# Front of a decoder-layer kernel: x tiles and weight blocks queued behind one another, six x tiles scaled on the vector engine

## What is computed

```
def rms_norm(x, g):
    y = xf * lax.rsqrt(jnp.mean(xf * xf, axis=-1, keepdims=True) + NORM_EPS)
    return (y * g.astype(jnp.float32)).astype(x.dtype)
...
u = rms_norm(h, norm_mix[i])
parts = jnp.split(u @ w_in[i], IN_OFFSETS, axis=-1)
q_n, kc, vc, ks_, vs_, kw, vw, gate_n, q_f, k_f, v_f, f_l = parts
o_n = nsa_attention(...)       # compressed, selected and window branches
o_f = forgetting_attention(...)
y = g_a * (o_n @ w_branch_nsa[i]) + g_b * (o_f @ w_branch_fox[i])
h = h + y @ w_out[i]
h = h + jnp.square(jax.nn.relu(v @ w_up[i])) @ w_down[i]
return rms_norm(h, norm_final)
```

## Time and profile before

| | us |
|---|---|
| time, median of 3 runs | 1181.09 (1180.12 to 1181.48) |
| time of the profiled execution | 1180.81 |
| its span on the slowest core (core 5) | 1179.2 |
| spans of the eight cores | 1175.8 to 1179.2 |
| PE busy | 1126.7 (96% of the span) |
| DVE busy | 653.2 (55%) |
| ACT busy | 623.1 (53%) |
| end of the front's last matmul on core 5 | 89.5 |

### The profile page before, as it was taken

One profiled execution on the slowest core, in us unless ns is written; L12 is line 12 of the kernel. 1 busy time (PEld: TensorE's weight loads), 2 busy tenths in 40 slices (PEclk: granted clock), 3 DMA queues, 4 the chain that ended last, 5 costly groups with the idle time before them and its releaser, 6 DMA issues.

```text
span 1179.2 us, 25453 instructions; the slowest of 8 cores (1175.8 to 1179.2 us)
## 1 busy us (share of the span) xinstructions
PE 1126.7 (96%) x8735; PEld 610.7 (52%) x8735; DVE 653.2 (55%) x1482; ACT 623.1 (53%) x1264; POOL 73.0 (6%) x136
## 2 busy tenths in 40 slices
PE   3888989999999999999999999999999999999997
PEld 2455655676575757644444455444444444444443
DVE  2555767655545455544344466356556564747377
ACT  4755888999999999932222366321111212030354
POOL 1000222122110000000000000000000000000000
PEclk9999999999999999999999999999999999999999
DMA  9963000002020034182032222312212111222034
GB/s 201 200 149 62 5 10 9 8 6 44 9 37 6 3 54 83 30 268 36 11 62 36 53 38 46 80 37 36 37 36 37 36 36 36 36 36 37 1 123 164
DMA packets 19228, 65.86 MB, mean 56 GB/s; under 512 B 4416, under 2 KB 5184, under 8 KB 15136
## 3 DMA queue, kind: packets, MB, share of 16 engines
q0 software_dynamic: 5184, 34.15, 16.8%
q1 hardware_dynamic: 13920, 30.08, 8.1%
HBM read 89.38 MB, written 8.39 MB: 83 GB/s over the span
## 4 chain that ended last, share of the span: by engine, by line
PE 89%; DMA 4%; DVE 3%; issue 2%; ACT 1%; DVEq 0%; POOL 0%; ACTq 0%; POOLq 0%; SPq 0%
PE bank L328 89%; DMA RG<-x 4%; DVE RG L328 2%; ACT RG L328 1%; POOL RG L328 0%; DVEq L167 0%; DVE arena L328 0%; DVEq L160 0%; DVE uT L328 0%; ACTq L167 0%; POOLq L167 0%; SPq L167 0%
## 5 line engine op out<-in xcount | busy, mean ns | idle before, releaser
L328 ACT ACTIVATE RG<-bank 128x512 bf16<-128x512 f32 (+3 forms) x888 | 452.0, 618 | 336.4 <-PE bank L328 331.5
L328 PE MATMUL bank<-uT,arena 128*128 128x512 bf16 x2048 | 490.3, 379 | 1.3 <-DVE arena L328 0.9
L328 PE MATMUL bank<-RG 128*128 128x65 bf16 (+8 forms) x3780 | 323.7, 225 | 14.0 <-DVE RG L328 11.2
L328 PEld LDWEIGHTS bank<-uT,arena 128*128 128x128 bf16 x2048 | 199.4, 98 | 213.4 <-issue 1.7
L328 DVE TENSOR_TENSOR RG<-RG,bank 128x512 f32<-128x512 f32 x320 | 218.9, 687 | 144.7 <-PE bank L328 141.5
L328 PE MATMUL bank<-arena,RG 128*128 128x512 bf16 x1280 | 279.5, 379 | 0.0
L328 PEld LDWEIGHTS bank<-RG 128*128 128x128 bf16 (+3 forms) x3780 | 198.7, 97 | 106.8 <-issue 21.9
L328 DVE TENSOR_TENSOR RG<-RG 128x512 bf16<-128x512 f32 (+3 forms) x199 | 118.3, 595 | 154.5 <-ACT RG L328 150.5
L328 PEld LDWEIGHTS bank<-arena,RG 128*128 128x128 bf16 x1280 | 124.8, 98 | 148.1
L328 ACT ACTIVATE RG<-RG 128x512 f32<-128x512 f32 (+3 forms) x149 | 86.8, 586 | 75.6 <-DVE RG L328 46.4
L328 ACT ACTIVATE RG<-bank,prm_s 128x512 f32<-128x512 f32 x64 | 43.9, 687 | 117.5 <-PE bank L328 114.8
(11 more groups left out here) (40 smaller groups left out, 296.8 us busy)
## 6 DMA issues: line engine op xcount, KB each, us to landing
arena<-wall POOLq DMA_DIRECT2D x30, 1024.0 KB, 9.8
RG<-x SPq DMA_DIRECT2D x32, 512.0 KB, 16.6
out<-RG SPq DMA_DIRECT2D x32, 256.0 KB, 2.1
RG<-c_qx SPq DMA_DIRECT2D x8, 144.0 KB
arena<-wall POOLq DMA_DIRECT2D x4, 256.0 KB, 16.1
RG<-wall POOLq DMA_DIRECT2D x1, 1024.0 KB, 13.9
arena<-wall POOLq DMA_DIRECT2D x1, 576.0 KB, 10.8
RG<-c_kx SPq DMA_DIRECT2D x4, 144.0 KB
```

Source lines behind the costliest of these rows:

```text
L328: return P.emit(eng, lambda e, method=method, kw=kw: getattr(e, method)(**kw), ins, outs, inc)
```

## The change

The x tiles are issued one by one by `load_x`. x1 goes ahead of the parameters. KV is issued once x3 has landed; x4 (and what stands behind it on SP) waits for the first piece of KV. QN waits for x10, x12 waits for QN, W1K waits for x12 with W1V behind it, and the constants wait for W1K. `stageA` and `stageB` run one tile less ahead. For tiles 0 to 5 the scale moves from ACT to DVE. Ln takes its epsilon from a small tile filled by a memset in place of `prm`. All four `kv_group`s of the first four tiles go in one piece (`room = 99.0` at i = 3), the later ones follow right behind their fourth tile, and qn groups move to tile 9 and on.

```diff
+        load_x(0)
+        W.pump(n=1)
+        load_x(1)
+        P.dma('sp', prm[:, :], prm_d)
+        load_x(2)
+        load_x(3)
...
+        E('dve', 'memset', ap=epsb[:, :], constant=1e-6)
...
-        E('dve', 'tensor_copy', out=w2b, in_=prm[:, 112:240])
-        E('dve', 'tensor_copy', out=posb[0:64, :], in_=prm[0:64, 48:112])
+        W.pump(n=2, after=[x_tok[3]])
+        load_x(4, [W.toks[1]])
+        load_x(5)
...
+            if i < 6:
+                E('dve', 'tensor_scalar', out=xn[i % 4], in0=xs[b], scalar1=rstd[:, i:i + 1], scalar2=None, op0=ALU.mult)
+            else:
+                E('act', 'activation', out=xn[i % 4], in_=xs[b], func=AF.Copy, scale=rstd[:, i:i + 1])
...
         stageA(0)
         stageB(0)
+        load_x(6)
         stageA(1)
-        stageB(1)
-        stageA(2)
         todo = []
         for i in range(16):
-            if i + 3 < 16:
-                stageA(i + 3)
             if i + 2 < 16:
-                stageB(i + 2)
-            if i == 4:
-                P.dma('pool', w1kb, wall_d[BLK['W1K']], after=[x_tok[7]])
+                stageA(i + 2)
+            if i + 1 < 16:
+                stageB(i + 1)
+            if i + 7 < 16:
+                load_x(i + 7, [W.toks[5]] if i == 5 else [])
+            if i == 3:
+                W.pump(n=3, after=[x_tok[10]])
             if i == 6:
-                W.pump(n=4, after=[x_tok[9]])
-            if i == 12:
-                late_consts()
+                w1k_tok = P.dma('pool', w1kb, wall_d[BLK['W1K']], after=[x_tok[12]])
+                W.pump(n=4)
+            if i == 9:
+                late_consts([w1k_tok])
             stageC(i)
+            if i == 8:
+                E('dve', 'tensor_copy', out=w2b, in_=prm[:, 112:240])
+                E('dve', 'tensor_copy', out=posb[0:64, :], in_=prm[0:64, 48:112])
             tg = i // 4
-            if i > 0:
+            if i % 4 > 0:
                 todo.append((1.0, lambda i=i: tm_group(i - 1)))
-            if i == 3 or i in (8, 12):
-                tg = (i - 1) // 4
+            if i % 4 == 3:
                 todo += [(1.73, lambda j=j, tg=tg: kv_group(tg, j)) for j in range(4)]
...
+                todo.append((1.0, lambda i=i: tm_group(i)))
...
-            room = 4.2
+            room = 99.0 if i == 3 else 4.4
```

More of the change, by code:

```diff
@@ L341, in build_program @@
         prm = sbt('prm_s', [128, 249], F32)
+        epsb = sbt('epsb', [128, 16], F32)
         RG_BYTES = 143552
@@ L375, in __init__ @@
                 self.released = set()
+                self.toks = []
             def slot_ap(self, pos):
@@ L385, in pump @@
                     for c0, c1 in PIECES.get(nm, [(0, 4096)] if nm in BLK else []):
-                        P.dma('pool', self.slot_ap(pos)[:, c0:c1], wall_d[BLK[nm], :, c0:c1], after=after)
+                        tok = P.dma('pool', self.slot_ap(pos)[:, c0:c1], wall_d[BLK[nm], :, c0:c1], after=after)
+                        self.toks.append(tok)
                     self.loaded += 1
@@ L465, in build_program, with load_x @@
         x_tok = []
[L466 to L473, removed]
+        def load_x(i, after=()):
+            x_tok.append(P.dma('sp', xs[i % NXS], x_d[i * 128:(i + 1) * 128, :], after=after))
+        load_x(0)
[4 more added lines that the diff above has]
+        load_x(3)
+        E('pool', 'memset', ap=identb[:, :], constant=1.0)
+        E('pool', 'affine_select', out=identb[:, :], in_=identb[:, :], pattern=[[1, 128]], compare_op=ALU.is_equal, fill=0.0, base=0, channel_multiplier=-1)
         for ap in (vall, fv0):
@@ L481, in build_program, with late_consts @@
         E('dve', 'memset', ap=ss, constant=0.0)
+        E('dve', 'memset', ap=epsb[:, :], constant=1e-6)
         E('act', 'activation', out=rstd[:, 0:1], in_=ss[:, 0, 0:1], func=AF.Ln, bias=1.0)
-        E('dve', 'tensor_copy', out=w2b, in_=prm[:, 112:240])
-        E('dve', 'tensor_copy', out=posb[0:64, :], in_=prm[0:64, 48:112])
-        def late_consts():
-            P.dma('sp', identf[:, :], cd['c_identf'])
+        W.pump(n=2, after=[x_tok[3]])
+        load_x(4, [W.toks[1]])
+        load_x(5)
+        def late_consts(after):
+            P.dma('sp', identf[:, :], cd['c_identf'], after=after)
             P.dma('sp', trib[:, :], cd['c_tri'])
@@ L535, in stageB @@
             tb = 3 + i % 3
-            E('act', 'activation', out=rstd[:, i:i + 1], in_=ss[:, i, 0:1], func=AF.Ln, scale=1.0 / D, bias=prm[:, 240:241])
+            E('act', 'activation', out=rstd[:, i:i + 1], in_=ss[:, i, 0:1], func=AF.Ln, scale=1.0 / D, bias=epsb[:, 0:1])
             E('act', 'activation', out=rstd[:, i:i + 1], in_=rstd[:, i:i + 1], func=AF.Exp, scale=-0.5)
-            E('act', 'activation', out=xn[i % 4], in_=xs[b], func=AF.Copy, scale=rstd[:, i:i + 1])
+            if i < 6:
+                E('dve', 'tensor_scalar', out=xn[i % 4], in0=xs[b], scalar1=rstd[:, i:i + 1], scalar2=None, op0=ALU.mult)
+            else:
+                E('act', 'activation', out=xn[i % 4], in_=xs[b], func=AF.Copy, scale=rstd[:, i:i + 1])
         def stageC(i):
@@ L571, in build_program @@
         stageB(0)
+        load_x(6)
         stageA(1)
[L573 to L574 removed]
         todo = []
         for i in range(16):
[L577 to L578 removed]
             if i + 2 < 16:
[L580 to L582 removed]
+                stageA(i + 2)
[5 more added lines that the diff above has]
+                W.pump(n=3, after=[x_tok[10]])
             if i == 6:
[L584 to L586 removed]
+                w1k_tok = P.dma('pool', w1kb, wall_d[BLK['W1K']], after=[x_tok[12]])
+                W.pump(n=4)
+            if i == 9:
+                late_consts([w1k_tok])
             stageC(i)
+            if i == 8:
+                E('dve', 'tensor_copy', out=w2b, in_=prm[:, 112:240])
+                E('dve', 'tensor_copy', out=posb[0:64, :], in_=prm[0:64, 48:112])
             tg = i // 4
[L589 removed]
+            if i % 4 > 0:
                 todo.append((1.0, lambda i=i: tm_group(i - 1)))
[L591 to L592 removed]
+            if i % 4 == 3:
                 todo += [(1.73, lambda j=j, tg=tg: kv_group(tg, j)) for j in range(4)]
[L594 to L596 removed]
+                todo.append((1.0, lambda i=i: tm_group(i)))
+                if tg == 1:
+                    todo += [(1.73, lambda c=c, tg=tg: qn_group(0, c, tg, ('act', 'dve'), front_bank)) for tg in range(2) for c in range(2)]
+            room = 99.0 if i == 3 else 4.4
             while todo and room > 0:
@@ L602, in build_program @@
             fn()
-        tm_group(15)
-        for j in range(4):
-            kv_group(3, j)
         W.release(pos_kv)
```

2 lines of the change are left out of this document (removed).

## The result

The changed kernel takes 1189.75 us (median of 6 runs) against 1181.21 for the kernel before (6 runs): ratio 1.0072, 95% interval 1.0060 to 1.0083. It is slower by 8.5 us, outside the range of the forecast (1177.8 to 1186.0). The profiled execution took 1190.03, 1.6 above the span of its slowest core, as before.

The account below looks back on a forecast made before the run. Late x transfers held the front, with 8.5 us of PE waits. Core 5: front end 88.5 plus 1089.7 gives 1178.2; slowest core 1180.6, plus 1.6 and 0.3, gives 1182.5 us; range 1177.8 to 1186.0.

Parts of the forecast that it names:

- The working's last step: Sum over cores: core 5 at 1178.2, core 0 at 1181.1, slowest core 1180.6, time 1182.5.
- Term 1: Start of front: x3 lands at 15.5, KV is issued then, its first piece takes 4.5 and lands at 20.0.
- Term 2: x4, issued at 20.0 behind KV's first piece: 3.7 alone plus 1.5 for neighbours, landing at 25.2 (bounds 23.7 and 27.4).
- Term 3: From x4's landing through ACT and DVE steps to the first kv group: 6.3, start at 31.5, a loss of 3.1.
- Term 4: PE waits behind the first kv group: 2.7 up to 46.8, then 0.7; 3.4 against the old 8.5.
- Term 5: PE's lower clock in the first kv groups: loss of 1.0, bounds 0 and 3.5; core 5's front ends at 88.5.
- What was to cost nothing: Later W1K, W1V, QN, constants, FOX0, SP's waits, memsets and casts: covered by other work, no cost beyond terms 1 and 2.
- (c): Rival, slower: idling ahead of tile 3 leaves PE at 1.2 GHz through four kv groups, price 3.5; 1185.8, chance 0.25.
- the sign for (c) at the end of the prediction: Sign in the new profile: the first kv groups take 7 us more than 7.
- (b): Rival, the order pays: x4 at 23.7, no lower clock, fewer waits, front end 85.0; 1178.6, chance 0.20.
- (a): Rival: the later start (3.1) and the removed waits (5.1) cancel on every core; 1181, chance 0.15.

Follow-up runs that it names:

- e6: Changed kernel with block KV in one 1,024 KB transfer in place of four of 256 KB, x4 waiting for all of it; 1191.21 us.
- e4: Changed kernel with the loop order turned round: stageC of the tile first, then stageB of the next, then stageA; all transfer waits kept; 1181.16 us.
- e1: Changed kernel without two waits: KV no longer waits for x3, nor x4 for KV's first piece; 1185.07 us.
- e2: Changed kernel with x4 no longer waiting for KV's first piece; KV still waits for x3; 1182.84 us.
- e9: e5 with two groups of keys and values ahead of tile 4's transposes and two behind (room = 4.4 throughout); 1176.98 us.
- e5: Changed kernel with e4's loop order and neither KV's wait for x3 nor x4's wait for KV's first piece; 1179.62 us.
- e7: Changed kernel with 32 extra matmuls, results unused, on PE in the wait ahead of tile 3's transposes; 1190.27 us.

## Why the prediction was wrong, by its own steps

The working gave core 5's front an end of 88.5; it was 94.1 there and 97.9 on core 2. On core 2 the 9.4 are 6.0 from the start of the first group (31.5 forecast, 37.48 measured), 2.0 from there to the second set (15.3 and the clock's 1.0 forecast, 18.27 measured), and 1.4 in the rest (40.7 forecast, 42.1 measured). The working's last step has a slip of its own: it put core 0 at 1181.1 and then the slowest core at 1180.6, with no reason for the 0.5; it does not bear on the miss.

**Term 1, the first piece of KV: mis-sized.** x3 landed at 16.3 (15.5 forecast), and the issue came 0.5 behind it. The piece then took 7.01 on core 2 in place of 4.5. The term got 4.5 from a whole block's 9.1 by counting data; the cores differ. The same part of the chain on core 3 and on core 5:

```profile
16.00 4.62 DMA arena<-wall
...
20.69 5.92 DMA RG<-x
```

```profile
16.32 4.81 DMA arena<-wall
...
21.20 7.82 DMA RG<-x
```

So 4.5 was right for these two and for cores 0 and 6 (4.6 and 4.7); cores 1, 2, 4 and 7 had 6.8 to 7.0, and three of them are the slowest of all. The metric is the slowest core. For a wait on the path of all eight cores, the price is that of the worst core, and the working took a middle.

**Term 2, x4: mis-sized.** 5.2 forecast (3.7 alone and 1.5 for its neighbours), with a bound of 3.7 plus 3.43; measured 5.92, 7.46 and 7.82 on cores 3, 2 and 5, and 5.4 to 8.7 over all eight. Even the bound, 7.1, was passed on four of them and reached on a fifth. The sentence that failed is "most of these pieces is through when x4's data begins". x4 was issued at 23.90 on core 2; the four pieces there, issued from 16.8 to 18.7, took up to 11.4 us, so the last came at about 30:

```profile
L150 POOL DMA_DIRECT2D arena<-wall x4: 535/655/882, 16.8 to 18.7; - x4
DMA to landing us min/median/max: 7.0/8.4/11.4
```

With no piece beside it x4 took 3.77 on this core (e6), the working's 3.7: the neighbours cost 3.7 there, not 1.5. Terms 1 and 2 together put x4's Square at 31.50 (25.2 forecast). Of the 6.3 between the two, 0.8 is x3, 0.5 the issue behind it, 2.5 the piece and 2.3 x4; on core 5, where it is 4.0, x4 has 2.6. The two trips together took 10.5 to 14.5 us on the eight cores, 9.7 forecast. Term 3 was 0.3 shorter than forecast, which leaves the 6.0 in the start of the first group.

**Term 3, from x4 to the first group: right.** 31.50 to 37.48 is 6.0, forecast 6.3. The scale, on VectorE of core 2, took 0.75 (0.7 forecast, 1.28 the bound):

```profile
33.23 0.75 DVE L328 TENSOR_SCALAR RG<-RG 128x1024 bf16<-128x1024 f32 x1 [11.60 <-ACT RG L328]
```

The bound of 1.28, from the form with two inputs, did not come into play. The Trainium skill (VectorE: DVE Perf Modes, The perf-mode tier table) has the 2× mode, two elements a cycle, for this form in float32, and this row agrees with it.

But term 3 was read too narrowly. It priced the chain from Square 4 and Exp 3 to scale 4 and multiplication 3 and took it as given; that this chain binds tile 3 to x4 at all was the most expensive fact of the change, as e4 shows (8.6 us with nothing else altered). The sum was right to let it pass to the end; the working never asked what the front would be without it.

**Term 4, the waits behind: mostly right.** Forecast 1.4 for tile 5, 0.65 for tm 4, 0.65 ahead of the next group; measured 1.45, 0.53 and 0.42. Not forecast was a wait of about 1 us of tile 7 for ScalarE on the cores at full clock (core 5):

```profile
49.88 0.61 PE L328 MATMUL bank<-identb,RG 128*128 128x128 bf16 x8 [0.99 <-ACT RG L328]
```

Nor were two of the three in the rest, 0.50 at 75.93 and 0.29 at 86.79 (0.42 at 89.91 was forecast as 0.7). On core 2 the rest is 1.4 us longer than forecast; these waits explain 0.5 of it, and the rows show no wait for the other 0.9. What the term replaced was mis-sized too, for most cores: the 8.5 of old waits are those of core 5, and core 2 had 58.7 - 52.6 = 6.1 of them.

**Term 5, the clock: right in size.** Core 5 had its first four groups at full speed:

```profile
35.25 7.07 PE L328 MATMUL bank<-uT,arena 128*128 128x512 bf16 x32 [0.25 <-DVE uT L328]
...
51.96 3.61 PE L328 MATMUL bank<-uT,arena 128*128 128x512 bf16 x16 [0.50 <-DVE uT L328]
```

Core 2 had 7.92 there and further slow pieces behind (2.04 at 49.41). To the second set it is 16.7 on the one and 18.3 on the other, 18.6 on core 4: the clock costs 0 to 1.9 by core, 1.0 was charged. The Trainium skill (TensorE: Matmul & The Clock Gate, HAM oscillation) says that a wait for a transfer throws TensorE back to the lower level. The 1.01 for the eight transposes behind the 11.11 us of idling on core 2 agrees with it.

**What was to cost nothing** cost nothing: from 36 to 130 us no instruction of TensorE, ScalarE or VectorE waited for a transfer on any core, so QN, W1K, W1V, the constants, FOX0 and the tiles behind x5 were all in time. Behind the front nothing changed.

**The rivals.** (c) had the right side, slower, and a fourth of the chance, but its mechanism was not this: TensorE was not at 1.2 GHz through four groups, 0.85 us came true on core 2 and 1.4 on core 4, and its x4 at 26 was 5 short. Its price of 3.5 was also half of what it describes: four groups of 1.73 at half speed cost 6.9 more, as the sign for (c) at the end of the prediction has it (7 us more). With 6.9 it would have stood at 1189.2, close to the measured time by luck. (b)'s turning point, x4 ahead of 23.7, is what e1 gives on core 2 (its Square at 23.07) and e2 on all cores (19.4 at the latest), and even those were slower than before: in e1 the first group waits for x5, in e2 KV comes late. (a)'s cancelling of gain and loss was the right shape with the wrong sizes: the loss at the start was 6.8 on core 5 and 8.3 on core 2, not 3.1, and the gain behind it 2.2 on the one and none on the other, not 5.1. The range was too narrow: it took the upper bound of x4 for its far end and had none for the piece ahead of it.

## What to carry to other kernels

A wait between two transfers costs a whole trip from issue to landing, here 4.6 to 7.0 us for 256 KB, 8.6 to 10.8 for 1,024 KB and 5.4 to 8.7 for the tile behind a piece, and two in series cost both; make sure that no more than one of them lies ahead of the first work, and price it by the worst core. Before transfers are put in the order of need, look at the order of the work on the engines: here a tile long in memory waited for the Square and scale of the next, and putting each tile's own steps first was worth as much as the whole loss. When a group of outputs blocks an engine, spread it: two groups on either side of the next tile's transposes took 3 us out of the front (e9 against e5).

## What the runs showed of the hardware

- A converting transfer of 256 KB issued into an empty queue takes 4.6 to 7.0 us by core, one of 1,024 KB 8.6 to 10.8 (e6); a plain tile of 512 KB beside the pieces 5.4 to 8.7, behind the whole block 3.4 to 7.4, where the first of the program took 3.7.
- After a dry spell the data rate came back slowly on core 2 of the changed kernel: no data from 16 to 19.5 us, though the first piece was issued at 16.81, then 29 to 193 GB/s over 4 us. The row has slices of half a microsecond from 15 to 35 us:

```profile
GB/s 57 16 0 0 0 0 0 0 0 29 78 78 57 106 131 143 193 193 152 176 176 135 115 168 152 201 213 242 344 361 262 320 361 287 320 336 328 361 303 360
```

- 32 matmuls that end 3.1 us ahead of the next work did not keep TensorE at its upper level (e7: 0.89 for eight transposes, 0.61 at full speed).
- Cores of one execution with the same program part ways by the clock: 7.07, 7.92 and 8.46 us on cores 5, 2 and 4 for the same 32 matmuls.
